# Two query quarters placed in the opening, and an eighth slot for expert rows in place of a half weight block kept in SBUF

## What is computed

```python
x = x + mixer_l(rmsnorm(x, g))          # l = 0 window attention, 1 gated short convolution, 2 two attentions with gates
h = rmsnorm(x, g2)
q = (h @ w_query).reshape(T, 8, 2, 128)             # 8 heads, two halves
s = einsum('thpd,hpnd->thpn', q, sub_keys)          # 128 keys per half
s_top, i_top = top_k(s, 16)                         # best 16 of each half
g_s, sel = top_k(sums of the 16 x 16 pairs, 16)     # 16 experts of 16384 per head
a = einsum('td,thkd->thk', h, expert_u[idx])        # 128 experts per token
x = x + einsum('thk,thkd->td', softmax(g_s) * gelu(a), expert_v[idx])
```

## Time and profile before

| | |
|---|---|
| Median of 3 runs | 2311.77 us (2311.58 to 2311.93) |
| The profiled execution | 2312.76 us |
| Its span, first to last instruction | 2310.8 us |
| Moved from and to HBM | 934.40 MB, mean 404 GB/s |
| PE, DVE, ACT, POOL busy | 80%, 72%, 40%, 39% of the span |
| Gathers, by 1 MB | 768 |
| Mean granted TensorE clock | 0.943 of full speed |

### The profile page before, as it was taken

The page is one execution under the profiler, slowest core; times in us unless marked ns, Lnnn a source line. Parts: engine busy times, 40 slices in busy tenths (PEclk is TensorE's granted clock), DMA queues, the critical chain, the costliest instruction groups (busy, mean ns, idle before and its releaser), DMA issues.

```text
span 2310.8 us, 21138 instructions
## 1 busy us (share of the span) xinstructions
PE 1852.7 (80%) x6234; PEld 949.1 (41%) x6234; DVE 1670.3 (72%) x3631; ACT 929.5 (40%) x2676; POOL 901.5 (39%) x772
## 2 busy tenths in 40 slices
PE   8987888877878777888868767887777878887876
PEld 5553344532646245435423333542334335432222
DVE  3487877878767876777877777678777767786545
ACT  3343663435314432333434452344253623444333
POOL 0143445424533443434435343334434334344432
PEclk8999989989998988999999989999989999999999
DMA  7399999999999999999999999999999999999997
GB/s 315 127 406 420 421 417 421 420 418 407 417 421 405 421 417 421 421 420 420 411 412 412 417 419 421 420 414 389 422 421 421 418 415 420 420 409 422 421 421 312
DMA packets 133368, 934.40 MB, mean 404 GB/s; under 512 B 15694, under 2 KB 16262, under 8 KB 21254
## 3 DMA queue, kind: packets, MB, share of 16 engines
q0 software_dynamic: 110592, 805.36, 84.4%
q1 hardware_dynamic: 22662, 127.71, 13.4%
HBM read 931.96 MB, written 1.05 MB: 404 GB/s over the span
## 4 chain that ended last, share of the span: by engine, by line
DMA 59%; PE 19%; DVE 8%; ACT 6%; issue 5%; POOL 2%; SPq 1%; DVEq 0%; ACTq 0%; POOLq 0%
DMA ring<-in_uv,idx 55%; PE y L1377 11%; DVE ring L1791 4%; PE acc L1256 3%; DMA wbuf<-in_wts 3%; POOL ring L1148 2%; DVE x L1782 2%; PE acc L1249 1%; ACT diag L1563 1%; ACT wgt L1553 1%; PE acc L1240 1%; ACT ge L1550 1%; ACT L1550 1%; PE y L1256 1%; PE tp L1306 1%
## 5 line engine op out<-in xcount | busy, mean ns | idle before, releaser
L1377 PE MATMUL y<-ring,diag 128*128 128x512 f32 x2288 | 1159.7, 639 | 353.3 <-ACT diag L1563 340.5
L1148 POOL DMA_INDIRECT ring<-in_uv,idx x768 | 901.3, 1174 | 1386.3 <-PE y L1377 936.0
L1791 DVE CUSTOM_DVE_ANT_0 ring<-ring,h 128x1024 f32<-128x1024 f32 x768 | 938.1, 1223 | 450.7 <-DMA ring<-in_uv,idx 448.5
L1377 PEld LDWEIGHTS y<-ring,diag 128*128 128x128 f32 x2288 | 414.1, 197 | 994.0 <-ACT diag L1563 641.9
L1550 ACT ACTIVATE ge<-a 128x1 f32<-128x1 f32 x768 | 155.3, 202 | 1174.3 <-DVE a L1791 1172.5
L1782 DVE SCALAR_TENSOR_TENSOR x<-ring,wgt,x 128x1024 f32<-128x1024 f32 x196 | 251.6, 1284 | 76.2 <-ACT wgt L1553 74.6
L1563 ACT ACTIVATE diag<-id_s,wgt 128x128 f32<-128x128 f32 x572 | 229.7, 402 | 18.8
L1553 ACT ACTIVATE wgt<-ge,gate 128x1 f32<-128x1 f32 x768 | 226.1, 294 | 25.2
L1256 PE MATMUL acc<-wbuf,fT 128*128 128x512 f32 (+1 forms) x304 | 149.9, 637 | 33.9 <-DMA wbuf<-in_wts 30.4
L1249 PE MATMUL acc<-fT,wbuf 128*128 128x128 f32 x896 | 113.2, 287 | 18.3 <-DMA wbuf<-in_wts 18.3
L1249 PEld LDWEIGHTS acc<-fT,wbuf 128*128 128x128 f32 x896 | 112.7, 203 | 33.8 <-issue 33.8
(11 more groups left out here) (187 smaller groups left out, 1288.4 us busy)
## 6 DMA issues: line engine op xcount, KB each, us to landing
wbuf<-in_wts SPq DMA_DIRECT2D x70, 1024.0 KB, 9.5
wkeep<-in_wts SPq DMA_DIRECT2D x22, 1024.0 KB, 17.9
ring<-in_uv,idx POOLq DMA_INDIRECT x768, 13.0
ring<-in_wts SPq DMA_DIRECT2D x6, 1024.0 KB, 10.1
caches<-in_wts SPq DMA_DIRECT2D x6, 1024.0 KB, 12.5
kbuf<-in_keys SPq DMA_DIRECT2D x24, 256.0 KB, 12.1
wbuf<-in_wts SPq DMA_DIRECT2D x4, 832.0 KB, 8.8
whalf<-in_wts SPq DMA_DIRECT2D x3, 1024.0 KB, 23.1
```

The lines of the kernel that those rows point to most:

```text
L1148: nc.gpsimd.indirect_dma_start(ring[:, n % RING, :], None, uv[layer(s)], bass.IndirectOffsetOnAxis(ap=idx[:, tile(s), k:k + 1], axis=0),). ...
L1377: mm = nc.tensor.matmul(y[half][:], diag[:, (d - 1) % DIAGS, :], ring[:, n % RING, D + half * BLK:D + (half + 1) * BLK], start=(k == y_end ...
L1791: ins = v.tensor_tensor_reduce(u, u, h[:, tile(s), :], 1.0, 0.0, ALU.mult, ALU.add, a[:, c:c + 1])
```

## The change

- `RING` is 8. `whalf` and its line in `KEPT` are gone: the first halves of q1, u1 and v are loaded for each tile through `wbuf`.
- Four items of the second tile's opening are no longer taken when they fit, but stand at fixed places of the main list (`PLACED`): its two turns behind the turn of q0, and two quarters of qkv0 behind the second scores. No other "ahead" item may go before a placed one.
- The square and the root of a mix or ffn norm on ACT are two items, so that others can stand between them.
- The constants are loaded behind the third qkv block.
- At the last step, adding the banks y to x may go ahead of a dot.

```diff
-RING = 7
+RING = 8
...
-def opening():
+def opening(alone):
...
     second = dense(1)
-    return (dense(0) + [x for x in second if x[1][1:3] not in ahead], [x for x in second if x[1][1:3] in ahead])
+    first, second = dense(0), [[x for x in second if (x[1][1:3] in ahead) == early] for early in (False, True)]
+    if not alone:
+        for item, follows in PLACED.items():
+            item = next(x for x in second[1] if x[1] == item)
+            second[1].remove(item)
+            first.insert([x[1] for x in first].index(follows) + 1, item)
+    return first + second[0], second[1]
+PLACED = {(1, "turn", "mix0", 0): (0, "turn", "win_q0", 0), (1, "turn", "mix1", 0): (1, "turn", "mix0", 0),
+          (1, "mm", "qkv0", 0): (0, "score", "win_s1", 0), (1, "mm", "qkv0", 1): (1, "mm", "qkv0", 0)}
...
-        [(0, "q1", 0), (1, "u1", 0), (2, "v", 0)],
...
-            if (s, name) == (0, f"qkv{QKV[1]}"):
+            if (s, name) == (0, f"qkv{QKV[2]}"):
                 out.append(("const", 0, "", 0))
...
-            if at is not None and (main is None or main + late[0] > max(at, free[engine]) + FITS * item[2]):
+            if dense_of[engine][0][1] not in PLACED and at is not None and (main is None or main + late[0] > max(at, free[engine]) + FITS * item[2]):
...
-                yield max(slot_free[n] for n in summed) + US["hop"], 0 if s < STEPS - 1 else 3, ("X", s)
+                yield max(slot_free[n] for n in summed) + US["hop"], 0, ("X", s)
...
-        whalf = sb("whalf", [P, PIECE])
```

More of the change, by code:

```diff
@@ L113 @@
 US = {"quarter": 1.95, "quarter_T": 2.05, "lat_part": 1.6, "small": 0.9, "branch": 0.95, "turn": 0.65, "gain": 2.0,
-      "score": 1.1, "av": 1.25, "key": 1.1, "take": 0.62, "rms": 1.65, "norm": 1.8, "sq": 1.45, "root": 0.35, "rope": 2.95,
+      "score": 1.1, "av": 1.25, "key": 1.1, "take": 0.62, "rms": 1.3, "norm": 1.8, "sq": 1.45, "root": 0.35, "rope": 2.95,
       "soft": 1.85, "exp": 0.41, "end": 1.75, "add": 0.75, "conv": 4.5, "gates": 1.45, "rope2": 5.2, "rope3": 3.5, "lat": 1.0,
@@ L169, in normed @@
         gain = [] if which == "mix" and s < TILES else [put("PE", "gain", which, US["gain"])]
-        h = put("DVE", "norm", which, US["norm"], *gain, put("ACT", "rms", which, US["rms"], x_ready, table="sqrt"))
+        h = put("DVE", "norm", which, US["norm"], *gain, put("ACT", "root", which, US["root"], put("ACT", "rms", which, US["rms"], x_ready), table="sqrt"))
         turns = [put("PE", "turn", f"{which}{i}", US["turn"], h) for i in range(2)]
@@ L380, in dense @@
     return out
-def opening():
-    ahead = [(kind, "mix") for kind in ("rms", "norm")]
+def opening(alone):
+    ahead = [(kind, "mix") for kind in ("rms", "root", "norm")]
     ahead += [(kind, f"mix{i}") for kind in ("turn", "copy") for i in range(2)]
@@ L566, in schedule @@
     done = {}
-    work, ahead = opening()
+    work, ahead = opening(planned is None)
     work += [x for s in range(2, STEPS) for x in dense(s)]
@@ L953, in build @@
         q_new, k_new = [big, qk], [h[:, 0, 768:], qk[:, D:1280]]
-        kept = [caches[:, 1040:1040 + WBLK], wkeep[:, 0, :], wkeep[:, 1, :], wkeep[:, 2, :], whalf[:],
+        kept = [caches[:, 1040:1040 + WBLK], wkeep[:, 0, :], wkeep[:, 1, :], wkeep[:, 2, :],
                 *(ring[:, 2 * i + 1:2 * i + 3, :].rearrange("p a n -> p (a n)") for i in range(3))]
@@ L1000, in build @@
         ffn_or_mix = [e for e in events("DVE", ("norm",)) if e[1] in ("mix", "ffn")]
-        sq_ready = Signal(sem("sq_ready"), [e for e in events("ACT", ("rms",)) if e[1] != "final"])
+        sq_ready = Signal(sem("sq_ready"), [e for e in events("ACT", ("root",)) if e[1] in ("mix", "ffn")])
         h_ready = Signal(sem("h_ready"), [(s, which + half) for s, which in ffn_or_mix for half in ("_half", "")])
@@ L1005, in build @@
         sq_done = Signal(sem("sq_done"), events("DVE", ("sq",)))
-        root_done = Signal(sem("root_done"), events("ACT", ("root",)))
+        root_done = Signal(sem("root_done"), [e for e in events("ACT", ("root",)) if e[1] not in ("mix", "ffn")])
         rope_done = Signal(sem("rope_done"), events("DVE", ("rope",)))
@@ L1506, in root_mean_square, with root_of_mean @@
                 mark(nc.scalar.activation(h[:, tile(s), :], x[:, tile(s), :], ACT.Square, accum_out=st[:, c:c + 1]))
+                if which == "final":
+                    root_of_mean(s, which)
+            def root_of_mean(s, which):
+                c = 10 * tile(s)
                 settle()
@@ L1576, in _ @@
                     root_mean_square(s, name)
+                elif kind == "root" and name in ("mix", "ffn"):
+                    root_of_mean(s, name)
                 elif kind == "root":
```

## The result

| | before | after |
|---|---|---|
| Median of 5 runs on one chip | 2311.63 us (2311.49 to 2311.93) | 2322.57 us (2321.27 to 2323.72) |
| Ratio, with its 95% interval | 1 | 1.0047 [1.0036, 1.0058] |
| The profiled execution | 2312.76 us | 2321.27 us |
| Its span | 2310.8 us | 2319.3 us |
| Moved from and to HBM | 934.40 MB | 937.54 MB |

The change makes the kernel **10.9 us slower** by the medians. The forecast was 2309.7, the range ended at 2319: the time lies outside, on the side to which I had given 0.22. The profiled execution of after is the fastest of its five, and the one of before lies 1.1 us above its median, so between the two traces there are only 8.5 us (2319.3 - 2310.8) to explain; the medians have some 2 us more.

A forecast was written before the change was run, and what follows sets the result against it. Transfers at 421 GB/s were taken to bound the kernel. Bytes +10.0, opening +0.9 and eighth slot -13 gave -2.1 on 2311.8, so 2309.7 us, called no change; 8-in-10 range 2301 to 2319.

The forecast's parts named there:

- What bounds the kernel: Whole run: transfers, not an engine, set the pace at 421 GB/s; some 16 us of tail follow the last transfer.
- The eighth slot, -13: Row gathers, 122.5 to 2290 us: one more in flight recovers 15.2 us of gaps, less 2 for new ones; bounds 0, -20.6.
- Rival (B): The slot buys little, as PE may wait for blocks streamed twice: recovery 4 us, 2318.7 us; chance 0.22.
- a long stretch under 418: Sign for Rival (B): mean GB/s from 122.5 to 2290 us under 418, against about 419.5 in the forecast.
- Bytes, +10.0: Weight loads: three more 1 MB loads, 7.5 us, and one block moved into the full stretch, 2.5 us; bounds 9.5 to 10.5.
- Constants, +2.6: Opening: masks land near 26 us, 4.3 us later, so PE waits for DVE before k's turn; bounds 0 to +3.2.
- what I set at 0 for the clock: PE clock in the opening: filler may keep it full, a new idle stretch may slow it; 0, bounds -1 and +3.
- Placed items: Opening on PE: the extra turn ahead of the first scores costs +0.7 us; the two qkv0 quarters cost nothing.
- Start of the rows, -2.6: First gathers, 95 to 122.5 us: earlier qkv1 and gather 7's own slot recover 2.6 us; bounds 0 and -3.1.
- rival (D): Placed quarters do nothing and the eighth slot alone closes the opening's gap: same time as forecast; chance 0.34 together with it.
- Opening in all, +0.9: Opening's sum: constants 2.6, turn 0.7, copy of qkv0 on ACT 0.2, start of the rows -2.6 us.
- Last rows, 0: End of the kernel: adding y to x before the last dot changes nothing; bounds -0.5 to +0.5 us.

The follow-up runs named there:

- e1: Kernel before without the kept half block (its three halves streamed for each tile), seven slots, old opening: 2319.22 us, ratio 1.0034.
- e2: e1 with RING = 8, so eight slots and the old opening: 2318.05 us, ratio 1.0031.
- e4: Kernel after, its gathers made to wait as if there were seven slots, order and loads unchanged: 2323.46 us, ratio 1.005.
- e10: Kernel before with only the last 24 gathers held to six in flight: 2312.06 us, ratio 0.9998.
- e6: Kernel after with three second-tile loads (first halves of q1, u1, v) cut to an eighth, all instructions kept: 2315.97 us, ratio 1.0015.
- e5: Kernel after with the constants loaded behind the second qkv block again: 2316.78 us, ratio 1.0022.
- e11: e8 with only the first turn placed; the second turn and two quarters taken when they fit: 2311.58 us, ratio 0.9997.
- e8: e3 with the constants loaded behind the second qkv block again: 2308.53 us, ratio 0.9989.
- e3: Kernel after with whalf, its line in KEPT and RING = 7 back, so only the opening is changed: 2313.39 us, ratio 1.0009.

## Why the prediction was wrong, step by step

**What bounds the kernel**: half right. The transfers do set the pace. But I read their pace from the mean of 16 engines, and took each low cluster for time that could be had back. I also read the 16 us from 2295 as a tail after the last transfer, when the last row landed only at 2299.9, 10.9 us before the end.

**The eighth slot, -13: the step that failed.** "The wire holds 2.49 us more in hand when a slot is late" was taken off nine clusters of the mean rate and gave 15.2. The clusters did shrink, by 5.4 us over the stretch, which is itself less than half. Of that the lag took 2.4 back, since a deeper ring lets the 15 quick engines run further ahead (4.7 us before, 6.8 after) while the last one sets every landing; in the largest cluster the landings had lost 1.1 us, not 4.4. Two pairs at the same order (e1 and e2, after and e4) put the slot at about 1 us, and e10 shows that a row of the lead is worth nothing at the end. Against the forecast that is 12 us, about the whole error (2322.6 - 2309.7 = 12.9). My lower bound, 0, was right; I gave it too small a chance, because the views I read (slices, windows of 7.5 us and more, gathers waiting for slots) all show the mean. The row that could have warned me was the last, 43 GB/s from 2295 to 2310.8: I booked it as "tail".

**Rival (B)** had the slot buy 4 us and gave 2318.7, nearest to the result, but for another reason. My sign for it, a long stretch under 418, did not come either: it read 418, between (B) and the 419.5 of the forecast. Its PE waits for streamed blocks did grow. The list of waits, after:

```profile
POOL ring L1154 <- PE y L1383: 943.7, 473, 11.4
...
PE acc L1262 <- DMA wbuf<-in_wts: 34.1, 12, 5.2
PE acc L1255 <- DMA wbuf<-in_wts: 29.2, 8, 12.6
...
PE acc L1239 <- DMA wbuf<-in_wts: 4.3, 2, 3.4
```

PE's three lines sum to 67.6 us, before to 53.4 (30.4, 18.3 and 4.7). But the long stretch became fuller, not emptier, and holding the ring to seven at the same loads (e4) cost only 1 us. GpSimd still waits some 940 us for PE: a ring that is full on the slow engine looks like that as well, so this list cannot tell a late slot from one that nobody needs.

**Bytes, +10.0**: borne out, though not to the 0.5 us of my bounds. e6 gave back 6.6 to 7.4 for 6.5, e1 cost 7.9 with 10.0 inside its interval. The one block moved behind the empty stretch shows in 343 for 364 GB/s.

**Constants, +2.6**: mechanism right, size too small, and above my bound of 3.2. The end of the program shows 4.6 and 5.8 us. Two parts: the masks landed at 27.3, not 26, because they came 3.8 us behind qkv1's second half (23.5), not the 2.2 to 3.2 us that I read from the earlier trace rows; the chain from the square on is then the 7.80 us of before (34.98 + 0.18 - 27.36), and the turn of k starts 4.1 us late. And PE's 4.77 us of idle time let the clock fall to 0.60 in 35 to 38.7, so that from the turn of k to the quarters it took 4.94 us in place of 3.84 in e5. Of what I set at 0 for the clock this is the part on the path, some 0.8 us at the indices (4.8 against 4.1).

**Placed items**: the extra turn was +0.6 (q1's turn at 39.29 in e5, 38.72 before), as I had it at +0.7. The quarters are hidden, as foretold, and better than nothing: they fill the idle stretch, the second scores take 1.71 us where they took 2.67 before, and without late constants the indices are 0.7 us sooner than before. The clock there read 0.50 in e11, after 3.54 us of idle PE, and 1.00 in e8 with the filler. The Trainium skill (TensorE: Matmul & The Clock Gate, Part 1) has activity release the slow clock; this pair agrees.

**Start of the rows, -2.6**: measured -2.5. Half of rival (D) falls: the placed quarters do something (e8 and e11). Its other half stands: the slot alone closes the gap at 115 us (e2), so in this kernel the -2.6 can't be put down to the quarters alone.

**Opening in all, +0.9**: measured +2.1 (e3, interval 0 to 4.2), inside which my two errors, constants too cheap and quarters too dear, partly cancel: that this sum came near is luck. **Last rows, 0**: right.

The measured parts are +7.9 (e1), +2.1 (e3) and -1 (slot), 9.0 in all, against 10.9 measured and intervals of 2 to 3 us each. Whether the rest is chance, the planner's new order or the parts meeting each other stays open.

## What to carry to other kernels

Price a gap in the transfers by the landing that ends last, not by the mean rate: look at the final microseconds for a line that falls to one sixteenth and stays. And before giving memory to another buffer, take one away with a stricter wait and see what it costs. Here a lag of one row (six in flight) left 12 us to gain and a lag of two rows (seven) only 1, while what the eighth slot displaced, 3 MB of reloads, was paid in full. And a small load for which the first instruction of a chain waits is worth keeping ahead of the large ones: here its place cost 4.6 to 5.8 us.

## What the runs showed of the hardware that I had not expected

- One of the 16 DMA engines ends 5.0 us (seven gathers in flight) to 7.4 us (eight) behind the mean of all. It is not slow there: its last eight packets take some 309 ns each, 26.5 GB/s, its full share of the pace. It is behind, and it was so for most of the run; no run shows where it lost the time. The Trainium skill (DMA: Bandwidth & Descriptors, Latency and other measured facts) says that engines 7 and 15 are usually slower than the rest. The trace agrees that one lags: before, the fifteenth signal of the last row comes 0.5 us behind the fourteenth and the sixteenth 3.5 us behind that. It does not tell which engine it is, nor why.
- Even the lagging engine does not keep the pace of clean windows. From the first gather (99.1) to the last landing (2308.4) the kernel after moved 937.5 - 17.2 = 920.3 MB in 2209.3 us, 416.6 GB/s over all; at 421 that would be 23 us less. If every engine carries a sixteenth of each load, as the last row shows for its last piece, the last one lost these too. No run here tells where, and the eighth slot gave back about 1 us.
- Small loads cost more than their bytes. The eight constants (0.27 MB, 0.6 us at 421) stand behind a block of weights, and the last of them lands 3.3 us behind it before (21.65 for 18.35) and 3.8 us after (27.33 for 23.51). Behind qkv1, in place of ahead of it, the masks came 5.6 us later (27.36 for 21.73 in e5, as the square shows), where the two halves put ahead of them are 2 x 2.49 = 5.0 us.
